# A hybrid decoder layer on one core: the second query block enters the opening, and the two parts of h become one product

## The chip, the cores and the metric

The kernel runs on one core of one Trainium2 chip. The metric is device time in microseconds (us); lower is better. Three runs of the kernel before gave 1751.47, 1755.07 and 1756.98 us, median 1755.07.

## The reference

One decoder layer for 256 tokens (two tiles of 128) of width 2048, all in float32. Cut to what matters here:

```python
mod = silu(c) @ w_ada + b_ada                       # w_ada is 2048 x 12288
sh1, sc1, g1, sh2, sc2, g2 = split(mod, 6)
h = rmsnorm(x, norm1_g) * (1 + sc1) + sh1
sq, sk, sv, cq, ckv, kr = split(h @ w_in, ...)      # 1024, 1024, 1024, 512, 256, 64 columns
sb_out  = stick_breaking_attention(sq, sk, sv)      # 8 heads of 128
q       = rmsnorm(cq) @ w_uq;  kv = rmsnorm(ckv) @ w_ukv
mla_out = mla_attention(q, kv, rope(kr))            # 8 heads
x = x + g1 * (concat(rmsnorm(sb_out), rmsnorm(mla_out)) @ w_o)
h2 = rmsnorm(x, norm2_g) * (1 + sc2) + sh2
x = x + g2 * peer_ffn(h2, ...)                      # top-16 experts of 16384 for 8 heads, gathered rows
return rmsnorm(x, final_norm_g)
```

`w_ada`, 100 MB, is read once. Its first two parts (sh1, sc1) are needed before h exists; the other four only later.

## The kernel before

Each engine runs one instruction list, written out in program order, and waits on semaphores. SP (SyncE) issues most loads, POOL (GpSimd) the late parts of `w_ada` and the expert gathers. Nothing is scheduled automatically; a few hand-written tables (`ada_after`, `ADA_IN`, `ADA_OUT`, `evicted`) say beside which weight pair some side work is done.

**The opening.** h can't be formed before sh1 and sc1 are known, and these need 33.5 MB of `w_ada`. So the kernel works in four quarters j of 512 columns. For each quarter the VectorE (DVE) adds up 16 pieces of 512 KB (`first_step`, lines 483 and 486: accumulator = piece times one value of c, plus accumulator). The TensorE (PE) then sums over partitions by products with a column of ones (`summed_columns`, line 498), DVE forms the shift and gain (`gained`), DVE and the ScalarE (ACT) apply them to four chunks of the transposed activations hT, and PE multiplies these four chunks with four chunks of `w_in` for every item of `OPENING`: the latents cq and ckv (line 876, h stationary) and the query block q0 (line 882, weights stationary). These are plain float32 products. The PSUM banks of the items stay open over the four quarters. `w_in` arrives in `opened` buffers, two sets of three, issued by SP among the pieces of `w_ada`. Between pieces 9 and 10 of the first quarter DVE also computes the angles of the rotary embedding (lines 1659 to 1677), and ACT takes their sine before it copies hT out of PSUM.

**The rest of the input projection.** The other items (q1, k0, k1, v0, v1, each 512 columns) come through two 32 KB ring slots in halves of 2 MB. Each item is worked in eight pairs of chunks (`Pair`). ACT casts a pair to a reduced float type (`make_high`, `win_high`, four buffers), DVE subtracts (`make_low`, line 452) and PE sums three products: high weights times high h, high weights times low h, low weights times high h. For q and k the weights are stationary and 256 tokens move (line 912, 24 products to a pair); for v the parts of h are stationary and 512 columns move (line 906, 12 to a pair). ACT may cast pair c only when PE has read pair c - 4. Beside these pairs DVE adds up the 16 pieces (1 MB each) of every later part of `w_ada` (`ada_sum`, line 322; three buffers, so POOL issues piece k when the sum of piece k - 3 is done). The table `ada_after` says after which pair. When 16 pieces are in, `ada_cols` on PE turns them into columns (line 333).

**Between projection and attention** PE transposes the latents, multiplies with `w_uq`, runs `ada_cols(3)`, then multiplies with `w_ukv`. DVE finishes pieces 59 to 63 before `ada_cols(3)`, and pieces 64 to 70 (up to `ADA_IN` = 71) before it may start on attention.

**Attention and output projection.** Sixteen half-head jobs run in a software pipeline; after the last one PE still sums squares for the group norm (`squares`, line 1030). The output projection is again eight pairs for each of four column blocks n (line 1069), with the same cast, subtract and multiply, and pieces 71 to 85 of `w_ada` are added on DVE, two of them before the first pair and none else in block n = 0. `rs_g` (line 1922) is the first step of the group norm on DVE; it waits for all squares.

**The retrieval** (from about 500 us on) gathers the experts' rows. The change touches nothing in it.

## Time and profile before

| | |
|---|---|
| median of 3 runs | 1755.07 us |
| the profiled execution | 1751.18 us |
| its span | 1749.4 us |
| PE busy | 1478.3 us (85%) |
| DVE busy | 1206.5 us (69%) |
| ACT busy | 542.8 us (31%) |
| POOL busy | 690.7 us (39%) |
| opening ends, projection by pairs starts | 149 us |
| projection ends | 268 us |
| first attention step of DVE | 313 us |
| output projection on PE | 363 to 462 us |

The shares are means over stages with different limits: in the opening the transfers run without a pause, in the projections PE does, and in the retrieval it is mostly the gathers. So a change in an early stage must be read from the waits of that stage. A busy PE is no PE at its peak, since its matmuls are pipelined. All times below are from the span's start.

### The profile page before, as it was taken

To read this page: it belongs to the slowest core of one execution; us is meant where nothing else is said; L and a number is where in the kernel's file an instruction comes from. 1 tells how busy PE (TensorE), PEld (TensorE's weight loads), DVE (VectorE), ACT (ScalarE), POOL (GpSimd) and SP (SyncE) were. 2 spreads that over 40 slices of the span, in tenths; PEclk is the share of its full clock that TensorE was granted. 3 is DMA by queue.
4 is the path that set the end of the run, shared out by engine and by line. 5 is a ranking of instruction groups with operands and counts; after the bars stand their busy time and mean duration, and the time that the engine had idled before them with its cause. 6 is when DMAs were issued, how large, how long until landed. Compare 5 with 4: busy or idle time off the path is not lost.

```text
span 1749.4 us, 20157 instructions
## 1 busy us (share of the span) xinstructions
PE 1478.3 (85%) x7320; PEld 980.5 (56%) x7320; DVE 1206.5 (69%) x2134; ACT 542.8 (31%) x1589; POOL 690.7 (39%) x626
## 2 busy tenths in 40 slices
PE   2979999989999998898999757656689899988874
PEld 2558987878788875666676434324333343333331
DVE  5877886879889988898454467768654555445463
ACT  3003442764311247343210146537421010101132
POOL 1000011000122354556676466555654454445461
PEclk9889999999999999999999876667789999998987
DMA  9999997849969679999999899998989999999996
GB/s 337 386 385 407 402 354 308 303 167 370 380 233 359 225 293 379 377 368 397 390 402 396 325 388 379 378 350 319 394 338 406 366 402 400 362 417 389 416 381 249
DMA packets 149806, 624.46 MB, mean 357 GB/s; under 512 B 33994, under 2 KB 38272, under 8 KB 86528
## 3 DMA queue, kind: packets, MB, share of 16 engines
q0 software_dynamic: 82976, 427.52, 62.6%
q1 hardware_dynamic: 66732, 195.67, 29.1%
q8 instruction: 58, 0.95, 0.2%
q14 instruction: 40, 0.33, 0.0%
HBM read 797.54 MB, written 2.10 MB: 457 GB/s over the span
## 4 chain that ended last, share of the span: by engine, by line
PE 31%; DMA 30%; DVE 24%; issue 6%; POOL 5%; ACT 3%; DVEq 1%; SPq 1%; POOLq 0%; ACTq 0%
DMA u_rows<-in_peer_u,expert 23%; DVE u_rows L2033 12%; PE ps L1167 6%; PE ps L1069 5%; PE ps L457 4%; PE ps L912 4%; DVE first_acc L486 3%; DMA v_rows<-in_peer_v,expert_rows 3%; POOL v_rows L801 3%; PE ps L906 2%; PE ps L1219 2%; PE ps L1134 2%; DMA ada_first<-in_w_ada 2%; PE ps L1204 2%; DMA u_rows<-in_peer_v,expert_rows 1%
## 5 line engine op out<-in xcount | busy, mean ns | idle before, releaser
L2033 DVE SCALAR_TENSOR_TENSOR u_rows<-u_rows,h 128x1024 f32<-128x1024 f32 (+1 forms) x416 | 595.3, 1469 | 377.9 <-DMA u_rows<-in_peer_u,expert 374.3
L801 POOL DMA_INDIRECT u_rows<-in_peer_u,expert x256 | 320.6, 1253 | 364.5 <-DVE u_rows L2033 289.5
L801 POOL DMA_INDIRECT v_rows<-in_peer_v,expert_rows x199 | 264.1, 1327 | 162.3 <-PE ps L1167 108.5
L1167 PE MATMUL ps<-v_rows,diag 128*32 128x512 f32 x1592 | 259.4, 693 | 65.1 <-DMA v_rows<-in_peer_v,expert_rows 35.6
L1219 PE MATMUL ps<-dense_rows,dense_weight 128*128 128x512 f32 x640 | 290.6, 612 | 14.9 <-DVE dense_sums L2112 8.2
L457 PE MATMUL ps<-h2T,dense_rows 128*128 128x256 f32 x1280 | 284.0, 383 | 4.2 <-ACT dense_weight L1565 4.1
L457 PEld LDWEIGHTS ps<-h2T,dense_rows 128*128 128x128 f32 x1280 | 243.4, 191 | 52.6 <-issue 17.9
L1219 PEld LDWEIGHTS ps<-dense_rows,dense_weight 128*128 128x128 f32 x640 | 123.1, 196 | 181.9 <-issue 174.9
L1167 PEld LDWEIGHTS ps<-v_rows,diag 128*32 128x32 f32 x1592 | 64.9, 125 | 182.5 <-issue 182.0
L308 POOL DMA_DIRECT2D ada_late<-in_w_ada x61 | 32.4, 531 | 303.7 <-DVE ada_acc L322 260.8
L1204 PE MATMUL ps<-high_hot,low_hot 128*128 128x40 f32 x512 | 82.1, 332 | 78.7 <-issue 54.0
L322 DVE SCALAR_TENSOR_TENSOR ada_acc<-ada_late,cact,ada_acc 128x2048 f32<-128x2048 f32 x57 | 133.8, 2348 | 18.8 <-DMA ada_late<-in_w_ada 17.7
L1167 PE MATMUL ps<-spare_rows,diag 128*32 128x512 f32 x296 | 135.7, 673 | 9.7 <-DMA v_rows<-in_peer_v,expert_rows 9.7
L1204 PEld LDWEIGHTS ps<-high_hot,low_hot 128*128 128x128 f32 x512 | 78.9, 244 | 95.0 <-issue 95.0
L1134 PE MATMUL ps<-h2T,ring 128*128 128x256 f32 x512 | 114.2, 383 | 0.0
L1134 PEld LDWEIGHTS ps<-h2T,ring 128*128 128x128 f32 x512 | 97.4, 192 | 13.0
L1487 ACT ACTIVATE hidden<-hidden 128x16 f32<-128x16 f32 x15 | 3.2, 215 | 314.6 <-DVE hidden L2041 311.5
L1576 ACT ACTIVATE low_hot<-iota,slot_rows 128x128 f32<-128x128 f32 x256 | 78.1, 387 | 41.1 <-PE ps L1204 40.9
L486 DVE SCALAR_TENSOR_TENSOR first_acc<-ada_first,cact,first_acc 128x1024 f32<-128x1024 f32 x60 | 77.0, 1284 | 16.1 <-DMA ada_first<-in_w_ada 10.8
L1509 ACT COPY weight_rows<-kept 32x4 f32<-32x4 f32 x240 | 47.1, 196 | 109.4 <-DVE kept L2058 106.7
L1561 ACT ACTIVATE diag<-ident,weight_rows 128x32 f32<-128x32 f32 x256 | 58.6, 308 | 40.0 <-PE ps L1167 39.4
L448 ACT CAST win_high<-ring 128x1024 fp32r<-128x1024 f32 x40 | 41.8, 1052 | 74.4 <-DMA ring<-in_w_in 32.0
(308 smaller groups left out, 1874.1 us busy)
## 6 DMA issues: line engine op xcount, KB each, us to landing
ada_late<-in_w_ada POOLq DMA_DIRECT2D x61, 1024.0 KB, 7.8
dense_rows<-in_dense_u SPq DMA_DIRECT2D x40, 1024.0 KB, 8.9
dense_rows<-in_dense_v SPq DMA_DIRECT2D x40, 1024.0 KB, 9.0
ada_first<-in_w_ada SPq DMA_DIRECT2D x64, 512.0 KB, 11.6
ring<-in_w_in SPq DMA_DIRECT2D x10, 2048.0 KB, 23.8
ring<-in_w_o SPq DMA_DIRECT2D x8, 2048.0 KB, 16.8
ring<-in_w_peer_q SPq DMA_DIRECT2D x8, 2048.0 KB, 13.8
opened<-in_w_in SPq DMA_DIRECT2D x8, 1024.0 KB, 13.0
```

The source lines that it names most:

```text
L322: nc.vector.scalar_tensor_tensor(out=a, in0=piece, scalar=cact[:, kc:kc + 1], in1=a, op0=ALU.mult, op1=ALU.add).then_inc(ada_steps, 1)
L457: ins = nc.tensor.matmul(half, lhs(k), rhs(k), start=(k == 0), stop=(k == kc - 1))
L486: nc.vector.scalar_tensor_tensor(out=a, in0=piece, scalar=cact[:, kc:kc + 1], in1=a, op0=ALU.mult, op1=ALU.add).then_inc(first_steps, 1)
L801: nc.gpsimd.indirect_dma_start(buf[:, :], None, table, bass.IndirectOffsetOnAxis(ap=places, axis=0), bounds_check=last_sparse, oob_is_err= ...
L912: ins = nc.tensor.matmul(banks[b // 2][:, T * (b % 2):T * (b % 2) + T], w.of(part, k, P * b, P), h[:, ch, :], start=first and b % 2 == 0, ...
L1069: ins = nc.tensor.matmul(banks[t], mixed[:, h, P * t:P * t + P], w.of(part, k), start=h % H == 0 and part is w.high and mixed is mix_high_ ...
L1134: ins = nc.tensor.matmul(bank[:, T * s:T * s + T], ring[item[name][0]][:, lo:lo + P], h2T[:, ch, :], start=(ch == 0 and s == 0), stop=(ch ...
L1167: ins = nc.tensor.matmul(ps[rows, k, :], diag[n % len(diag)][:, :], v_slot(n)[0][:, 512 * k:512 * k + 512], start=first, stop=last)
L1204: ins = nc.tensor.matmul(o, low_hot[i % 2][:, k, :], high_hot[i % 2][:, k, :], start=True, stop=True)
L1219: ins = nc.tensor.matmul(ps[:, 4 + t, :], weight_tile(PIECE * m + a)[:, P * t:P * t + P], rows[:, 512 * a:512 * a + 512], start=m == 0 and ...
L1576: ins = nc.scalar.activation(hot[:, k, :], iota128[:, :], ACT.Abs, scale=-1.0, bias=slot_rows[:, 1, BATCH * b + k:BATCH * b + k + 1])
L2033: ins = nc.vector.scalar_tensor_tensor(out=u_rows[b][:, lo:hi], in0=u_rows[b][:, lo:hi], scalar=1.0, in1=h2[:, q // H, lo:hi], op0=ALU.mul ...
```

## The change

What it does:

- q1 joins `OPENING`. Its products are plain float32 and are issued after those of q0 in each quarter (16 more in each). Its weights get four buffers of their own (`opened_late`, in ring slot 0), so they are loaded among the pieces of `w_ada`. Only k0, k1, v0 and v1 are left for the pairs: 32 pairs in place of 40.
- All eight PSUM banks are now taken by the opening's items, so the column sums go into 32 columns of the bank of ckv that its 320 columns leave free.
- `hT_high` and `hT_low` are two halves of one tile `h_parts`. For k0 and k1 one product with 512 moving columns (high and low h side by side) takes the place of two with 256. The two results stand in the two halves of a bank, each block of 128 output rows has its own bank, and DVE adds the halves when it evicts (`heads_out`, a reduction), where ACT copied before.
- The rotary angles move on DVE from the first quarter into the second one's pieces, and the sine on ACT after the second quarter's h.
- `ADA_IN` is 67 (was 71). Of the pieces 32 to 85, DVE does 3 before the first pair (was 2), 18 beside the pairs (was 25), 11 after the last pair (was 5), 3 before attention (was 7) and 19 in the output projection (was 15): three of the four added there stand in block n = 0, one in n = 1.
- The squares of the last two jobs are summed on PE after the first two pairs of the output projection, no longer before it.

```diff
-    OPENING = ("cq", "ckv", "q0")
+    OPENING = ("cq", "ckv", "q0", "q1")
-    ADA_IN, ADA_OUT = 71, 86
-    ada_after = {c: (37 + (c - 4) * 11 // 18, 37 + (c - 3) * 11 // 18) for c in range(4, 22)}
-    ada_after.update({c: (48 + (c - 25) * 11 // 15, 48 + (c - 24) * 11 // 15) for c in range(25, 40)})
+    ADA_IN, ADA_OUT = 67, 86
+    ada_after = {c: (35 + c * 13 // 22, 35 + (c + 1) * 13 // 22) for c in range(22)}
+    ada_after.update({c: (48 + (c - 25) * 5 // 7, 48 + (c - 24) * 5 // 7) for c in range(25, 32)})
...
     def first_bank(j):
-        return ps[:, 7 - j % 2, :]
+        return ps[:, unit["ckv_0"][0], 512 - 2 * KC:512]
...
+                            else:
+                                for b in range(4):
+                                    if part is w.high:
+                                        ins = nc.tensor.matmul(banks[b].rearrange("p (s n) -> p s n", s=2), w.of(part, k, P * b, P),
+                                                               h_parts[:, :, ch, :], start=first, stop=False, skip_group_check=True)
+                                    else:
+                                        ins = nc.tensor.matmul(banks[b][:, 0:T], w.of(part, k, P * b, P), hT_high[:, ch, :],
+                                                               start=False, stop=last, skip_group_check=True)
...
-            for k in range(JOBS + 6):
+            for k in range(JOBS + 4):
                 for stage, j in steps(k, (0, scores), (6, squares), (4, values), (2, middle)):
                     stage(j)
...
+                    if n == 0 and m < 2:
+                        squares(JOBS - 2 + m)
                     if n == 0 and m == 1:
                         gate_rows()
...
+            def heads_out(name, b):
+                dst = sbq if name[0] == "q" else sbk
+                parts = full(dve, f"{name}_{b}").rearrange("p (s n) -> p n s", s=2)
+                empty(nc.vector.tensor_reduce(dst[:, 4 * int(name[1]) + b, :], parts, AX.X, ALU.add), f"{name}_{b}")
...
+                    if n in (1, 2) and 3 <= m < 7:
+                        heads_out(IN_ITEMS[3 + n][0], m - 3)
...
-            ada_sums(59, 64)
+            ada_sums(53, 64)
...
-                    if (n, m) in ((1, 0), (1, 1), (1, 2), (1, 6), (1, 7), (2, 0), (2, 1), (2, 6), (2, 7), (3, 0), (3, 1), (3, 2), (3, 3)):
+                    if (n, m) in ((0, 3), (0, 6), (0, 7), (1, 0), (1, 1), (1, 2), (1, 3), (1, 6), (1, 7), (2, 0), (2, 1), (2, 6), (2, 7), (3, 0), (3, 1), (3, 2), (3, 3)):
                         ada_sum(next(ada))
```

Where instructions moved, first on DVE in the first quarter of the opening, before (`trig` is the rotary table, `first_acc` the accumulator; the numbers behind names count tiles):

```order
L486 SCALAR_TENSOR_TENSOR first_acc_77<-ada_first_72,cact,first_acc_77 128x1024
L1659 CAST st<-posi 128x2
L1661 TENSOR_SCALAR trig<-trig,st 128x32 x2
L1668 TENSOR_SCALAR trig<-trig 128x64
...
L1677 TENSOR_SCALAR trig<-trig 128x64
L486 SCALAR_TENSOR_TENSOR first_acc_77<-ada_first_73,cact,first_acc_77 128x1024
```

and now:

```order
L496 SCALAR_TENSOR_TENSOR first_acc_76<-ada_first_71,cact,first_acc_76 128x1024
L496 SCALAR_TENSOR_TENSOR first_acc_76<-ada_first_72,cact,first_acc_76 128x1024
...
L1711 TENSOR_TENSOR modc<-ps,vcA 128x2x4
L1715 SCALAR_TENSOR_TENSOR a1c<-modc,vcA 128x4
...
L496 SCALAR_TENSOR_TENSOR first_acc_77<-ada_first_75,cact,first_acc_77 128x1024
L1682 CAST st<-posi 128x2
L1684 TENSOR_SCALAR trig<-trig,st 128x32 x2
```

The rotary steps stood between two pieces of the first quarter and now stand behind the first shift and gain (`modc`, `a1c`), among the pieces of the second quarter.

Next on DVE where the output projection begins, before (`mix_low_part` is the low part of the attention output, `wo_high` the cast weights, `rs_g` the group norm):

```order
L452 TENSOR_TENSOR ring_low_119<-ring_49,wo_high_124 128x1024
L1922 TENSOR_SCALAR rs_g<-ps 128x4
L1874 TENSOR_TENSOR mix_low_part<-mix,mix_high_part 128x512
L452 TENSOR_TENSOR ring_low_119<-ring_49,wo_high_125 128x1024
L1874 TENSOR_TENSOR mix_low_part<-mix,mix_high_part 128x512
L452 TENSOR_TENSOR ring_low_119<-ring_49,wo_high_126 128x1024
L1874 TENSOR_TENSOR mix_low_part<-mix,mix_high_part 128x512
L452 TENSOR_TENSOR ring_low_119<-ring_49,wo_high_123 128x1024
```

and now:

```order
L460 TENSOR_TENSOR ring_low_122<-ring_49,wo_high_127 128x1024
L1948 TENSOR_SCALAR rs_g<-ps 128x4
L1900 TENSOR_TENSOR mix_low_part<-mix,mix_high_part 128x512
L460 TENSOR_TENSOR ring_low_122<-ring_49,wo_high_128 128x1024
L1900 TENSOR_TENSOR mix_low_part<-mix,mix_high_part 128x512
L460 TENSOR_TENSOR ring_low_122<-ring_49,wo_high_129 128x1024
L323 SCALAR_TENSOR_TENSOR ada_acc<-ada_late_89,cact,ada_acc 128x2048
L1900 TENSOR_TENSOR mix_low_part<-mix,mix_high_part 128x512
L460 TENSOR_TENSOR ring_low_122<-ring_49,wo_high_126 128x1024
```

`rs_g` keeps its place behind the second pair, and a piece of `w_ada` has come in behind the fourth.

Last on PE at the same place, before (`sq` holds the squares, line 1044 the rows of g1):

```order
L1030 MATMUL ps<-ones,sq 128x1 x4
L1069 MATMUL ps<-wo_high_123,mix_high_part 128x512 x2
...
L1069 MATMUL ps<-ring_low_119,mix_high_part 128x512 x4
L1069 MATMUL ps<-wo_high_124,mix_high_part 128x512 x2
...
L1069 MATMUL ps<-ring_low_119,mix_high_part 128x512 x4
L1044 MATMUL ps<-ident,modc 128x128 x16
```

and now:

```order
L1084 MATMUL ps<-wo_high_126,mix_high_part 128x512 x2
...
L1084 MATMUL ps<-ring_low_122,mix_high_part 128x512 x4
L1045 MATMUL ps<-ones,sq 128x1 x2
L1084 MATMUL ps<-wo_high_127,mix_high_part 128x512 x2
...
L1084 MATMUL ps<-ring_low_122,mix_high_part 128x512 x4
L1045 MATMUL ps<-ones,sq 128x1 x2
L1059 MATMUL ps<-ident,modc 128x128 x16
```

The last squares, for which `rs_g` waits, now come behind the products of the second pair.

## Rows read from the trace of the kernel before

**Rows 1.** Busy time by stretch: all engines, granted clock, DMA share, GB/s.
```profile
100.00:120.00 20.00, 18.62 (x63) 12.04 (x61) 16.08 (x14) 0.00 (x0) 0.00 (x0) 0.94 1.05 386
```
**Rows 2.** PE in order of time, opening: start, us, line, operation, idle before.
```profile
40.44 3.57 PE L498 MATMUL ps<-ones,first_acc 128*128 128x1 f32 x16 [5.83 <-DVE first_acc L486]
45.55 14.15 PE L876 MATMUL ps<-opened,hT 128*128 128x512 f32 x32 [1.53 <-DVE hT L1732]
...
66.94 1.95 PE L498 MATMUL ps<-ones,first_acc 128*128 128x1 f32 x16 [0.34 <-DVE first_acc L486]
70.20 13.11 PE L876 MATMUL ps<-opened,hT 128*128 128x512 f32 x32 [1.32 <-DVE hT L1732]
83.15 7.07 PE L882 MATMUL ps<-hT,opened 128*128 128x256 f32 x32
...
123.55 3.57 PE L498 MATMUL ps<-ones,first_acc 128*128 128x1 f32 x16 [4.93 <-DVE first_acc L486]
128.72 13.53 PE L876 MATMUL ps<-opened,hT 128*128 128x512 f32 x32 [1.59 <-DVE hT L1732]
```
**Rows 3.** DVE in order of time, opening.
```profile
27.81 0.16 DVE L1659 CAST st<-posi 128x2 f32<-128x2 int32 x1
...
32.15 8.23 DVE L486 SCALAR_TENSOR_TENSOR first_acc<-ada_first,cact,first_acc 128x1024 f32<-128x1024 f32 x6
...
109.71 13.78 DVE L486 SCALAR_TENSOR_TENSOR first_acc<-ada_first,cact,first_acc 128x1024 f32<-128x1024 f32 x10 [2.60 <-DMA ada_first<-in_w_ada]
```
**Rows 4.** The chain that ended last, in order of time: start, us, what.
```profile
149.15 66.23 PE ps L912 x552
215.38 3.84 PE ps L333 x32
219.22 5.33 PE ps L912 x24
224.55 43.65 PE ps L906 x191
...
291.95 3.48 PE ps L333 x32
...
371.48 3.57 PE ps L1044 x32
375.05 46.31 PE ps L1069 x204
```
**Rows 5.** A reduction of 512 PSUM columns on DVE, in order of time.
```profile
534.22 0.69 DVE L1999 TENSOR_REDUCE halves<-ps 128x32 f32<-128x512 f32 x1
```
**Rows 6.** DVE in order of time, end of the projection.
```profile
252.09 2.35 DVE L452 TENSOR_TENSOR ring_low<-ring,win_high 128x1024 fp32r<-128x1024 f32 x2
...
259.29 2.35 DVE L322 SCALAR_TENSOR_TENSOR ada_acc<-ada_late,cact,ada_acc 128x2048 f32<-128x2048 f32 x1 [1.45 <-DMA ada_late<-in_w_ada]
...
282.78 2.35 DVE L322 SCALAR_TENSOR_TENSOR ada_acc<-ada_late,cact,ada_acc 128x2048 f32<-128x2048 f32 x1 [0.21 <-DMA ada_late<-in_w_ada]
```
**Rows 7.** PE in order of time, first scores of attention.
```profile
310.00 0.60 PE L988 MATMUL ps<-sbq,sbk 128*128 128x256 f32 x2
```
**Rows 8.** DVE in order of time, before attention.
```profile
310.66 2.35 DVE L322 SCALAR_TENSOR_TENSOR ada_acc<-ada_late,cact,ada_acc 128x2048 f32<-128x2048 f32 x1 [0.43 <-DMA ada_late<-in_w_ada]
312.93 0.55 DVE L1810 SCALAR_TENSOR_TENSOR za<-za 128x384 f32<-128x384 f32 x1
```
**Rows 9.** DVE in order of time, output projection.
```profile
364.86 0.15 DVE L1922 TENSOR_SCALAR rs_g<-ps 128x4 f32<-128x4 f32 x1
...
376.29 0.69 DVE L1874 TENSOR_TENSOR mix_low_part<-mix,mix_high_part 128x512 fp32r<-128x512 f32 x1 [6.07 <-ACT mix_high_part L1434]
...
383.51 1.23 DVE L452 TENSOR_TENSOR ring_low<-ring,wo_high 128x1024 fp32r<-128x1024 f32 x1 [1.37 <-ACT wo_high L448]
...
414.69 2.35 DVE L322 SCALAR_TENSOR_TENSOR ada_acc<-ada_late,cact,ada_acc 128x2048 f32<-128x2048 f32 x1 [1.93 <-DMA ada_late<-in_w_ada]
416.96 3.49 DVE L452 TENSOR_TENSOR ring_low<-ring,wo_high 128x1024 fp32r<-128x1024 f32 x3
```

More of the change, by code:

```diff
@@ L327, in ada_sums, with ada_bank @@
             ada_sum(k)
+    def ada_bank(part):
+        return ps[:, 3 if part == 2 else 7, :]
     def ada_cols(part):
@@ L701, in _ @@
                 if j < 3:
-                    for i in range(9, KC):
+                    for i in range(12, KC):
                         first_load(sp, KC * (j + 1) + i)
-            for name, col, width in IN_ITEMS[3:]:
-                if name == IN_ITEMS[4][0]:
+            for name, col, width in IN_ITEMS[4:]:
+                if name == "k0":
                     sp.wait_ge(first_steps, 4 * KC)
@@ L859, in _ @@
                 fill(ins, f"xT{u}")
+            banks = {name: [take(pe, f"{name}_{i}") for i in range(2)] for name in OPENING}
             summed_columns(0)
-            banks = {name: [take(pe, f"{name}_{i}") for i in range(2)] for name in OPENING}
             for j in range(4):
@@ L876, in _ @@
                                 ins = nc.tensor.matmul(banks[name][t][:, 0:width], hT[:, ch, P * t:P * t + P], w[:, ch % 4, 0:width],
-                                                       start=(ch == 0), stop=last)
+                                                       start=(ch == 0 and (name, t) != ("ckv", 0)), stop=last, skip_group_check=True)
                                 if last:
@@ L890, in _ @@
                     summed_columns(j + 1)
-            for n, (name, _, width) in enumerate(IN_ITEMS[3:]):
-                banks = [take(pe, f"{name}_{i}") for i in range(2)]
+            for n, (name, _, width) in enumerate(IN_ITEMS[4:]):
+                banks = [take(pe, f"{name}_{i}") for i in range(2 if name[0] == "v" else 4)]
                 for m in range(PAIRS):
@@ L1746, in _ @@
                 if j:
[L1747 removed]
+                    opened_read_through(dve, j - 1, 3)
                     h_parted(j - 1)
@@ L1751, in _ @@
                         first_step(j + 1, kc)
+                        if j == 0 and kc == 11:
+                            trig_args()
                 else:
                     opened_read_through(dve, 3, 0)
-                    ada_sums(32, 34)
-            for n, (name, _, width) in enumerate(IN_ITEMS[3:]):
+                    ada_sums(32, 35)
+            for n, (name, _, width) in enumerate(IN_ITEMS[4:]):
                 for m in range(PAIRS):
```

149 lines of the change are left out of this document (76 added, 73 removed).

## The prediction

> **What bounds the kernel now.** I read the stretches first, then the chain of waits, then each engine in order of time where the change touches it. Three stages matter.
>
> The opening, 7 to 149 us, runs at the pace of its transfers: the DMA share is 1.05 at 386 GB/s [rows 1]. PE is idle before every quarter's column sums, 4.93 us before the last ones, and always until DVE has added its last piece [rows 2]; DVE in turn waited 2.60 us for a piece, then added ten in a row [rows 3]. So a load that is put in front of a piece delays the end of the stage, while more products on PE cost nothing as long as they fit into the gap.
>
> The projection, 149 to 268 us, belongs to PE: on the chain stand 576 products of 256 columns, 16 ones-products and 192 products of 512 columns without a wait [rows 4]. DVE keeps up with it, and also loses time to late pieces there [rows 6].
>
> From 268 to 462 us PE and DVE take turns. Attention begins when DVE is through its pieces of `w_ada` [rows 8], and the output projection is PE's again, with DVE close behind it [rows 4, 9]. The retrieval after that is untouched and follows the shift of its start, so I cost it at nothing.
>
> The sum is made against the profiled execution: span 1749.4 us, time 1751.18, so 1.8 us lie around the span. The median of the runs shown is 3.9 us above it. I add the change to the median.
>
> **The opening, with the rotary steps moved: ends 14.0 us later.** First the start. The six last pieces of the first quarter start at 32.15 where the rotary steps began at 27.81 [rows 3]. These steps leave, and so does ACT's wait for them before it copies hT. The column sums can start 4.3 us earlier than at 40.44, the first products at 41.2 in place of 45.55 [rows 2]. The pieces must have landed for that, which I take since six were then added without a wait. The moved steps fall beside PE's first quarter, where DVE has room.
>
> Now PE's pace. A quarter took 12.95 us for the latents (70.20 to 83.15) and 7.07 us for a query block; between the end of the products and the next quarter lie 3.6 us (0.3 to the column sums, then 66.94 to 70.20) [rows 2]. With two query blocks a quarter costs 12.95 + 14.14 + 3.6 = 30.7 us, the first one 31.9 (its latents took 14.15 us). From 41.2 the quarters start at 73.1, 103.8 and 134.5.
>
> And the transfers' pace. Three chunks of q1 (1.05 MB each) come ahead of the last piece: 3.15 MB at 386 GB/s are 8.2 us. The last column sums go from 123.55 to 131.7 at the earliest, the last quarter from 128.72 to 136.9, or 135.3 if PE is not slowed by its gap. Both paces come out within 2 us of each other; I take the slower one, 136, and 27.1 us of products: the opening ends at 163.1, before it ended at 149.15. Ends: 161.6 (PE alone) and 166 (both add up in part). h_parts for the last quarter and the casts of k0 run beside the next pairs, four of which are ready ahead; its weights wait, as before, for the last piece, and have 30 us to land.
>
> **The projection: 24.6 us shorter on PE.** q1 leaves it. 552 products of 256 columns took 66.23 us, 0.120 us each [rows 4]; q1 has 192: 23.0 us. In k0 and k1, 128 products of 512 columns replace 256 of 256. The v products took 43.65 us for 192, 0.227 us each, so the doubled width costs 0.107 us more and each product has 0.013 us that doesn't depend on width: 128 times 0.013 is 1.6 us saved. No row shows a moving operand in two pieces. If it streams like one, the gain is 1.6; if at half rate, 128 times 0.227 = 29 us are lost. Every operand here is read at the column rate, so I take 1.6 and keep the 29 for a rival. The Trainium skill (TensorE: Matmul & The Clock Gate, Back-to-back issue gap) puts the width-free part of a product at about 2.5 ns; by that figure the merge would save 0.3 us (an estimate from that page) and the forecast would be 1.3 us higher. The row's 13 ns disagrees with it here.
>
> Together: 14.0 - 23.0 - 1.6 = **-10.6 us** when the v products end, at 257.6.
>
> **DVE beside it: 0.** A pair costs DVE 1.16 us, a piece 2.27 (414.69 to 416.96) [rows 9]. With 13 pieces to 22 pairs that is 2.50 us to a pair. The reductions that replace ACT's copies are 8; the nearest row is a reduction of 512 PSUM columns in 0.69 us [rows 5], between 0.6 and, if the stride of 256 halved its rate, 1.4. Four to eight pairs make 0.35, in all 2.85 us against PE's 64 x (0.227 + 0.120) / 8 = 2.78. DVE falls back 0.1 us a pair over 16 pairs, and the cast buffers give it a lead of four pairs less some 3 us. Hidden; 0 to +4 if it isn't.
>
> **`ada_cols(3)`: +1.5.** PE reached it at 291.95, 23.7 us after the v products [rows 4]; the last piece was done at 285.13 [rows 6], 6.8 us in hand. Now PE arrives at 281.3. DVE leaves the pairs near 251 (the four pairs it is ahead by, less the cast), with 11 pieces to add, not 5: at 2.35 us each done at 277, at the pace of the last eight before (259.29 to 285.13, 3.23 us each, limited by landing) at 286.5. So 0 to +5.2. Loads are no more in total, hence a value near the lower end.
>
> **The start of attention: -1.5.** PE had the first scores at 310.6 [rows 7]; with one scaling on ACT between, for which I put 0.8 us, DVE could begin at 311.4. It began at 312.93, straight after a piece [rows 8]. Three pieces stand there now, all loaded during the wait for `ada_cols(3)`; what is late next is the scores. Running sum -10.6.
>
> **The output projection: +6.0, given back.** DVE did `rs_g` at 364.86 [rows 9]. Its wait is new in kind: the last squares stand behind PE's second pair, which ended at 371.48 [rows 4]. `rs_g` is held for 6.9 us, and behind it on DVE stand the low parts of all further pairs. PE itself isn't stopped, since the 3.57 us of g1 rows cover the third pair. Then come four pieces, 9.1 us, before pair 18. Of these 16.0 us, DVE's idle stretches take up 6.07, 1.37 and 1.93 [rows 9], and the margin of pair 18 takes 0.5 (low part ready near 418.1; PE's 17 pairs from 375.05 take 46.31 us, 2.72 each, so it started it at 418.6). Left are 16.0 - 9.4 - 0.5 = 6.1, less a little where g1's rows shift too: 6.0. The column sums behind pair 18 give DVE room again, but it then ran as tightly as before, so nothing of it comes back. Bounds: 0, if DVE's lead is larger than I read it, to +8, if the wait for the transfer isn't absorbed. The squares leaving the end of attention give nothing: DVE's two pieces set that start.
>
> **Sum.** -10.6 + 1.5 - 1.5 + 6.0 = **-4.6 us**: 1746.6 on the profiled execution, **1750.5 us** on the median.
>
> **Rivals.**
> - *Nothing is given back.* The output projection stays PE's, as 9.4 us of idle DVE would suggest at first sight; against it speaks the margin of 0.5 us at pair 18. -4.6 - 6.0 = -10.6: 1744.5 us.
> - *Small waits eat the rest.* Pieces land every 3.23 us as they did at the end of the projection: +3.7 at `ada_cols(3)`, and 2 us in the pairs and the opening. +1.1: 1756.2 us. For it: DVE waited for pieces in all three stages [rows 3, 6, 9]. Against: the bytes are the same.
> - *DVE becomes the bound of the projection, and the kernel slower.* Place: the 17 pieces between the pairs from the end of the opening on. If each waits 1.45 us, as the one at 259.29 did [rows 6], that is 24.6 us; the lead of the cast buffers takes 8.5: +16.1, in sum +11.5: 1766.6 us. It decides from (9.9 + 8.5) / 17 = 1.1 us a piece. Against it: before, most pieces there came without a wait, though the queues were as full.
> - *The two-piece operand streams at half rate:* -4.6 + 29 + 1.6 = +26: 1781 us. It is slower from 0.08 us a product.
>
> **Numbers.** 0.3% is 5.3 us, about what a measurement of this kernel tells from no change. My own forecast 0.49, with its own range 1746 to 1754; it straddles the bound, so 0.26 of it is faster and 0.23 within. No giveback 0.18 (faster), small waits 0.20 (within), DVE bound 0.10 and half rate 0.03 (slower). Faster 0.44, same 0.43, slower 0.13. The range reaches past both near rivals, and part of the way to the third: 1741 to 1761.
>
> **What would show it.** Opening: first latents at 41, quarters near 73, 104 and 136, products of q1 ending near 163; a last quarter after 140 breaks that step. Projection: 128 products of 512 columns at 0.227 us for k0 and k1, no idle PE up to 258; idle PE until `ring_low` means DVE is the bound. `ada_cols(3)` at 281 to 287, first DVE step of attention near 302. Output projection: `rs_g` waiting near 7 us for the squares, and PE idle for 0.5 to 0.8 us before pairs 11 to 18, 6 us in all. If those idles are absent, the gain is the full one.

## The result, and the profile after

The changed kernel takes 1769.52 us (median of 4 runs, 1766.57 to 1776.05), the kernel before 1753.69 us (4 runs): ratio 1.0094, 95% interval [1.0066, 1.0121]. It is slower by 0.9%, where 1750.5 us and a range up to 1761 had been forecast. The profiled execution (span 1774.3 us) is the slowest of the four, 6.5 us above their median. Its span is 24.9 us longer than that of the trace before; 17.4 of these have arisen when the retrieval begins and 7.5 lie in the retrieval, which the change doesn't touch. So stages are compared only up to its start.

The opening, PE in order of time, against [rows 2] (start, us, line, operation, idle before):

```profile
41.19 13.76 PE L885 MATMUL ps<-opened,hT 128*128 128x512 f32 x32 [1.52 <-DVE hT L1753]
...
72.72 3.15 PE L508 MATMUL ps<-ones,first_acc 128*128 128x1 f32 x16 [3.96 <-DVE first_acc L496]
77.19 12.83 PE L885 MATMUL ps<-opened,hT 128*128 128x512 f32 x32 [1.32 <-DVE hT L1753]
...
137.02 13.11 PE L885 MATMUL ps<-opened,hT 128*128 128x512 f32 x32 [1.59 <-DVE hT L1753]
149.96 7.07 PE L891 MATMUL ps<-hT,opened 128*128 128x256 f32 x32
156.87 7.07 PE L891 MATMUL ps<-hT,opened_late 128*128 128x256 f32 x32
```

It starts at 41.19 and ends at 163.6, as forecast (41.2 and 163.1). In between, the second quarter is late, 77.2 for 73.1, since PE waited 3.96 us for its last piece; the other two start at 106.8 and 137.0 for 103.8 and 136. The transfers are as full as in [rows 1]:

```profile
100.00:120.00 20.00, 18.68 (x68) 11.96 (x67) 13.33 (x16) 2.12 (x4) 0.00 (x0) 0.91 1.05 385
```

From the end of the pairs to attention, PE, against [rows 4, 7]:

```profile
258.86 1.03 PE L941 MATMUL ps<-ident,lat 128*128 128x128 f32 x8
...
293.83 6.96 PE L337 MATMUL ps<-ones,ada_acc 128*128 128x1 f32 x32 [11.29 <-DVE ada_acc L323]
300.65 9.46 PE L465 MATMUL ps<-ckvT,ring 128*128 128x256 f32 x32
309.95 7.03 PE L465 MATMUL ps<-ring,ckvT 128*128 128x512 f32 x16
316.81 1.04 PE L994 MATMUL ps<-ident,qpe 128*128 128x128 f32 x8
317.69 0.60 PE L1003 MATMUL ps<-sbq,sbk 128*128 128x256 f32 x2
```

The pairs end at 258.9 (before 268.3): 9.4 us gained. Then PE waits 11.3 us for the last piece that part 3 of `w_ada` needs. After the wait even its own work is slower. In the kernel before, the same column sums took 3.63 us and the first `w_ukv` products 7.15, here 6.96 and 9.46; before:

```profile
291.78 3.63 PE L333 MATMUL ps<-ones,ada_acc 128*128 128x1 f32 x32
295.27 7.15 PE L457 MATMUL ps<-ckvT,ring 128*128 128x256 f32 x32
```
 The granted clock of the changed kernel shows why (columns as in [rows 1]; of the last three the first is the clock, as a share of full speed):

```profile
280.00:285.00 5.00, 2.54 (x6) 0.76 (x4) 4.18 (x2) 0.00 (x0) 0.53 (x1) 0.98 0.92 331
285.00:290.00 5.00, 0.00 (x0) 0.00 (x0) 2.87 (x2) 0.00 (x0) 1.06 (x2) 0.50 0.91 339
290.00:295.00 5.00, 1.17 (x6) 1.20 (x6) 3.60 (x5) 0.00 (x0) 0.53 (x1) 0.50 0.77 275
295.00:300.00 5.00, 5.00 (x25) 5.00 (x25) 3.39 (x9) 0.00 (x0) 0.00 (x0) 0.50 0.65 213
```

0.50 is the lower of the two levels, 1.2 GHz. The clock fell to it while PE was idle and rose again only after 305 us.

DVE beside it, against [rows 6, 8]: the pieces come at the pace of their landing, eleven of them take 39.9 us from 253.76 on, 3.63 us each, and attention waits for the scores:

```profile
271.32 2.35 DVE L323 SCALAR_TENSOR_TENSOR ada_acc<-ada_late,cact,ada_acc 128x2048 f32<-128x2048 f32 x1 [5.15 <-DMA ada_late<-in_w_ada]
...
291.33 2.35 DVE L323 SCALAR_TENSOR_TENSOR ada_acc<-ada_late,cact,ada_acc 128x2048 f32<-128x2048 f32 x1 [2.21 <-DMA ada_late<-in_w_ada]
...
319.07 0.56 DVE L1836 SCALAR_TENSOR_TENSOR za<-za 128x384 f32<-128x384 f32 x1 [11.86 <-ACT za L1385]
```

A good half of the wait has its cause further back, as e5 shows. Between 228 and 236 us the transfers almost stop:

```profile
220.00:228.00 8.00, 8.00 (x40) 6.68 (x39) 6.45 (x6) 5.08 (x7) 0.53 (x1) 1.00 1.03 406
228.00:236.00 8.00, 8.00 (x39) 7.13 (x39) 2.50 (x3) 0.43 (x1) 0.53 (x1) 0.64 0.13 42
```
```profile
231.94 0.17 DVE L347 TENSOR_TENSOR modc<-ps,vcA 128x16 f32<-128x16 f32 x1 [5.20 <-PE ps L337]
```

DVE has added piece 47, casts up to pair 25 and then waits 5.2 us for `ada_cols(2)`, before which it may not begin the next part. All three piece buffers are full, and both ring slots wait for PE. In the kernel before DVE waited 2.57 us for the same sums, but the transfers went on at 383 GB/s from 212 to 228 us.

The output projection, against [rows 9] (waits: engine, what, releaser, us in all, times, longest), and PE's longest wait behind the first pair (the 4.5 us stand before that pair):

```profile
PE ps L1084 <- DVE ring_low L460: 9.4, 10, 4.5
...
DVE rs_g L1948 <- PE ps L1045: 6.9, 1, 6.9
```
```profile
412.00 0.70 PE L1084 MATMUL ps<-wo_high,mix_high_part 128*128 128x512 f32 x2 [1.94 <-DVE ring_low L460]
...
435.39 4.03 PE L337 MATMUL ps<-ones,ada_acc 128*128 128x1 f32 x32
```

From its first product to the end of the last key rows it takes 110.0 us (369.5 to 479.5), before 98.8 (363.35 to 462.1).

The balance up to the retrieval, after minus before: end of the pairs -9.4; wait for the piece +11.3; column sums and first `w_ukv` products at the lower clock +3.3 and +2.3; start of attention behind the scores -1.5; output projection +11.2. These terms make +17.2. The transposes behind it begin at 483.7 against 466.3: **+17.4 us**. The medians differ by 15.8.

### The profile page after: what moved, and what is told of

Read it like the earlier page. It is cut to its first block, busy times and chain, and to the rows that moved or that the text cites. A ratio compares the mean times of both kernels' runs of the same rounds, so it can differ in the third digit from the quotient of the medians.

```text
span 1774.3 us, 19763 instructions
## 1 busy us (share of the span) xinstructions
PE 1488.6 (84%) x7128; PEld 978.6 (55%) x7128; DVE 1202.5 (68%) x2134; ACT 534.1 (30%) x1577; POOL 692.5 (39%) x626
## 4 chain that ended last, share of the span: by engine, by line
PE 26%; DMA 24%; DVE 14%; issue 6%; POOL 6%; ACT 1%; DVEq 1%; POOLq 0%; ACTq 0%
DMA u_rows<-in_peer_u,expert 16%; DVE u_rows L2059 8%; PE ps L1184 8%; PE ps L1236 7%; DMA v_rows<-in_peer_v,expert_rows 5%; POOL v_rows L811 4%; PE ps L465 3%; PE ps L1084 2%; PE ps L1151 2%; PE ps L1221 2%; POOL u_rows L811 1%; DMA ada_late<-in_w_ada 1%; DMA u_rows<-in_peer_v,expert_rows 1%; DVEq L1979 1%; DVE tk_i L1987 1%
## 5 line engine op out<-in xcount | busy, mean ns | idle before, releaser
L811 POOL DMA_INDIRECT u_rows<-in_peer_u,expert x256 | 324.3, 1267 | 366.6 <-DVE u_rows L2059 291.4
L1236 PE MATMUL ps<-dense_rows,dense_weight 128*128 128x512 f32 x640 | 288.8, 609 | 15.8 <-DVE dense_sums L2138 9.2
L1184 PE MATMUL ps<-spare_rows,diag 128*32 128x512 f32 x296 | 139.7, 694 | 9.5 <-DMA v_rows<-in_peer_v,expert_rows 9.5
L1184 PEld LDWEIGHTS ps<-spare_rows,diag 128*32 128x32 f32 x296 | 29.7, 125 | 53.1 <-issue 52.9
```

What stands on the lines that cost most here:

```text
L811: nc.gpsimd.indirect_dma_start(buf[:, :], None, table, bass.IndirectOffsetOnAxis(ap=places, axis=0), bounds_check=last_sparse, oob_is_err= ...
L1184: ins = nc.tensor.matmul(ps[rows, k, :], diag[n % len(diag)][:, :], v_slot(n)[0][:, 512 * k:512 * k + 512], start=first, stop=last)
L1236: ins = nc.tensor.matmul(ps[:, 4 + t, :], weight_tile(PIECE * m + a)[:, P * t:P * t + P], rows[:, 512 * a:512 * a + 512], start=m == 0 and ...
```

## Experiments

The marks of the kernels that were run more than once, from their traces (us). "Stage" is from the end of the pairs to DVE's first attention step; "w_o" from the output projection's first product to the last key rows; "retrieval" is when the transposes ahead of it begin. The marks show more than the medians can, since the retrieval's own length varied by over 10 us between traces (1277.8 us in e5, 1290.6 in the changed kernel). But each kernel has one trace, and the end of the pairs alone differs by up to 5 us between kernels that are alike up to there, so a difference of a few us between two rows is not shown to come from the edit. The ratio is to the kernel before on the same chip, whose medians were 1752.27 (e1 to e4), 1748.40 (e5 to e8), 1754.15 (e9 to e12) and 1753.57 us (e13, b1).

| kernel | pairs end | PE waits | column sums, next products | first step | stage | w_o | retrieval | ratio, 95% |
|---|---|---|---|---|---|---|---|---|
| before | 268.3 | 0 | 3.63, 7.15 | 312.9 | 44.7 | 98.8 | 466.3 | 1 |
| after | 258.9 | 11.3 | 6.96, 9.46 | 319.1 | 60.2 | 110.0 | 483.7 | 1.0094 |
| e1 sums last | 255.6 | 5.4 | 3.63 | 310.2 | 54.6 | 108.4 | 474.6 | 1.0067 [1.0041, 1.0094] |
| e2 squares back | 254.9 | 11.3 | 6.96, 8.94 | 314.6 | 59.7 | 106.5 | 475.6 | 1.0096 [1.0065, 1.0128] |
| e3 pieces back | 259.8 | 12.0 | 6.96, 8.89 | 320.2 | 60.4 | 100.4 | 475.2 | 1.0036 [1.0011, 1.0062] |
| e4 small fill | 256.5 | 0.7 | 5.17, 9.03 | 313.7 | 57.2 | 107.5 | 475.9 | 1.0094 [1.0064, 1.0124] |
| e5 first sums early | 257.2 | 4.9 | 6.96, 9.61 | 311.2 | 54.0 | 108.3 | 474.1 | 1.0101 [1.0061, 1.0141] |
| e6 sums between | 258.1 | 3.8 | 6.96, 9.67 (wide) | 311.0 | 52.9 | 108.5 | 474.1 | 1.0050 [1.0029, 1.0070] |
| e9 joined, two back | 263.9 | 0 | 3.63, 8.81 (wide) | 309.6 | 45.7 | 102.3 | 466.4 | 0.9989 [0.9966, 1.0012] |
| e12 joined, four back | 257.5 | 0 | 4.69, 9.48 (wide) | 312.7 | 55.2 | 98.5 | 467.2 | 1.0025 [0.9999, 1.0050] |
| e13 e9, sums spread | 260.7 | 1.7 | spread | 318.7 | 58.0 | 103.9 | 478.1 | 1.0067 [1.0043, 1.0091] |
| b1 before, sums spread | 268.8 | 0 | spread | 322.9 | 54.1 | 98.5 | 477.4 | 1.0072 [1.0047, 1.0097] |

"Wide" are the 16 products of 512 columns, 7.03 us at full clock.

**The wait ahead of `ada_cols(3)`: e1, e6.** PE waits there for DVE's last piece, and everything behind it waits too.

```diff
 # e1: behind both halves of the w_ukv products; e6: between them
-            ada_cols(3)
             w = group(pe, "w_ukv", 2 * n_in, KVR // P)
             ...
+            ada_cols(3)
```


> The changed kernel, with `ada_cols(3)` moved on PE behind the `w_ukv` products. Theory (the column sums wait for late pieces, and everything behind them with them): PE goes from `w_uq` to `w_ukv` without a wait at about 282.5 and is through near 296, the column sums wait little, the first scores come near 302 and DVE's first attention step, after its last three pieces, near 307.5 instead of 319.1. The kernel gains 11 to 12 us on the changed kernel: about 1758 us. Rival 1 (DVE's own pieces and rotary work set the start of attention anyway): the start moves by 5 us or less, 1764 to 1768. Rival 2 (the loss at this place is given back later): the start moves by 11 us and the time by less than 5.

The stage got 5.6 us shorter, not 11, near rival 1 in size; 1763.86 us. The mechanism is another one than rival 1 had. PE found a new wait, for banks that DVE's rotary work held, and DVE then waited 9.5 us for the sums:

```profile
291.59 8.82 PE L465 MATMUL ps<-ring,ckvT 128*128 128x512 f32 x16 [5.41 <-DVE rt L1815]
300.25 3.63 PE L337 MATMUL ps<-ones,ada_acc 128*128 128x1 f32 x32
303.74 1.07 PE L994 MATMUL ps<-ident,qpe 128*128 128x128 f32 x8
```


> The changed kernel, with `ada_cols(3)` between the two halves of the `w_ukv` products (behind the 32 of 256 columns, ahead of the 16 of 512). Where the sums stood behind both halves, the second half waited 5.4 us for banks that DVE's rotary work held, and DVE then waited 9.5 us for the sums. Theory (both waits come from that order alone): PE waits about 4 to 5 us for the sums, the second half runs beside the rotary work, the first attention step comes 46 to 48 us after the end of the projection's pairs, where the changed kernel has 60.2, the order with the sums last 54.6 and the kernel before 44.7: about 1757 us. Rival (what is missing is the pieces' landing): 54 us again, 1764.

52.9 us, 7.3 less than after and 5 to 7 more than expected. Both waits went as foreseen (PE 3.8 us, DVE 2.3), but the clock fell behind the 3.8 us just as behind 11.3: 6.96 us for the sums, 9.67 for the wide products. The lower clock costs 6.0 us here, about the size of the miss. Median 1758.98 us (about 1757 expected).

**The pause of the transfers: e5.**

```diff
-                    if w.c == 22:
+                    if w.c == 20:
                         copied(pe, "k0_3")
                         ada_cols(2)
 # DVE: ada_finish(2) at pair 23, pieces 48 to 54 beside pairs 24 to 31, ada_sums(55, 64) behind
```


> The changed kernel, with `ada_cols(2)` on PE two pairs earlier (after pair 20, when its last piece has been added), and the first pieces of the next part from pair 24 on, 7 of them beside the pairs in place of 5. Theory (the transfers stood still from 228 to 236 us because all three buffers of `w_ada` were full and DVE waited for these column sums; that pause, and not DVE's work, is why piece 63 comes 8 us later than in the kernel before): the pause goes or shrinks to 3 us, the last piece ahead of `ada_cols(3)` is done 5 to 6 us earlier, PE's wait there shrinks from 11.3 us to 5 or 6, attention starts as much earlier: 1762 to 1764 us. Rival (the pieces come at the pace of the queue and the pause is made up behind it): the last piece moves by 2 us or less and the time stays within 2 us of 1769.5.

The theory on the pause holds in the trace. The same stretch moved 189 GB/s in place of 42, and PE's wait shrank by 6.4 us, from 11.29 to 4.89. What is left of it has the pieces' pace: the last eleven took 38.3 us here too, 3.48 us each, from 247.3 on.

```profile
228.00:236.00 8.00, 8.00 (x34) 6.54 (x33) 6.09 (x5) 3.16 (x3) 1.06 (x2) 0.92 0.60 189
```
```profile
285.76 6.96 PE L337 MATMUL ps<-ones,ada_acc 128*128 128x1 f32 x32 [4.89 <-DVE ada_acc L323]
```

The stage is 6.2 us shorter and the retrieval begins 9.6 us earlier (1.7 of it from pairs that ended earlier). The time doesn't show it: the median is 1767.35 us (1762 to 1764 expected) and the ratio, 1.0101, no better than the changed kernel's 1.0094. The five runs reach from 1753.62 to 1771.39 us, and the profiled one is the fastest.

**The output projection: e2, e3.**

```diff
 # e2
-            for k in range(JOBS + 4):
+            for k in range(JOBS + 6):
 ...
-                    if n == 0 and m < 2:
-                        squares(JOBS - 2 + m)
```


> The changed kernel, with the last two `squares` back at the end of attention, so that `rs_g` doesn't wait. Theory (the 6.9 us in which `rs_g` holds DVE are paid by PE later in the output projection, because DVE's slack is used up by the four more pieces): the output projection gets 5 to 7 us shorter up to pair 18, less 0.5 at its start: about 1764 us. Rival (the wait is absorbed by DVE's idle time, the loss comes from the four pieces alone): 0 to -2, 1768 to 1770.

w_o 106.5: 3.5 us shorter, between the theory (5 to 7) and the rival (0 to 2). `rs_g` doesn't wait, but PE still idles before seven pairs. Median 1768.65 us, which is the rival's number (1768 to 1770) and not the theory's 1764.

```diff
 # e3
-    ADA_IN, ADA_OUT = 67, 86
+    ADA_IN, ADA_OUT = 71, 86
-                    if (n, m) in ((0, 3), (0, 6), (0, 7), (1, 0), (1, 1), (1, 2), (1, 3), (1, 6), ...
+                    if (n, m) in ((1, 0), (1, 1), (1, 2), (1, 6), ...
```


> The changed kernel, with the four pieces of `w_ada` that it added to the output projection's block 0 and 1 back ahead of attention (`ADA_IN` 71). Theory: ahead of attention they fit into the time in which DVE waits for the first scores (it was idle from 307 to 317.7, four pieces cost 9.1 us), so attention starts at most 1 us later; in the output projection DVE gets 9.1 us of slack and PE's idle before pairs 11 to 18 disappears: -8 to -9 us, about 1761 us. Rival 1 (`rs_g`'s wait alone makes the idle): -2 or less, 1767 to 1770. Rival 2 (the pieces land too late ahead of attention, at 3.6 us each): attention starts 4 to 5 us later, in sum -4.

The theory came true. Attention starts 0.2 us later relative to the pairs (its four pieces were added while DVE waited for the scores), w_o is 9.6 us shorter, and PE waits before no pair but the first:

```profile
317.13 2.35 DVE L323 SCALAR_TENSOR_TENSOR ada_acc<-ada_late,cact,ada_acc 128x2048 f32<-128x2048 f32 x1 [0.46 <-DMA ada_late<-in_w_ada]
320.18 0.56 DVE L1836 SCALAR_TENSOR_TENSOR za<-za 128x384 f32<-128x384 f32 x1 [0.70 <-ACT za L1385]
```

Median 1760.88 us (about 1761 expected). With both edits (e12) w_o is 98.5 us, the 98.8 of before: the four pieces and the squares are the whole loss there, the pieces the larger part.

**The clock behind the wait: e4, e7, e11.** In all three PE does work in the wait whose result nobody reads.

```diff
 # e4: 44 products of 128 x 128; e7: 12 of 128 x 512 with cqT; e11: 14 of these
             copied(pe, "v1_1")
+            for _ in range(44):
+                nc.tensor.matmul(ps[:, 7, 128:256], ident[:, :], ident[:, :], start=True, stop=True)
             ada_cols(3)
 # e11 also: no row of sums, but two of them behind each group of four first w_ukv products
```


> The changed kernel, with 44 idle products (128 x 128, on a bank that nobody reads) on PE in the 11.3 us in which it waits for the pieces ahead of `ada_cols(3)`. The output is the same. Theory (the idle stretch lowers the granted clock, and the column sums and the `w_ukv` products behind it run slowly for that alone): the column sums take 3.6 to 4.4 us instead of 6.96, the products of `w_ukv` 7.2 to 7.5 instead of 9.46, the first scores come 4 to 5.5 us earlier: about 1764.5 us. Rival (they are slow for another reason, such as loads that collide with them): the durations stay and the time stays within 1 us of 1769.5.

> The changed kernel, with 12 idle products of 128 x 512 (the shape of the `w_uq` products before them) in PE's wait ahead of `ada_cols(3)`. With 88 small ones there the clock stayed at 1.00 in the gap and still fell to 0.55 to 0.77 behind it. Theory (the small products don't keep the clock up, the wide ones do): column sums 3.6 us, `w_ukv` products 7.15 and 7.03, the stage from the pairs' end to the first attention step 54 to 55 us in place of 60.2. Rival (the clock falls behind the gap whatever fills it, with the column sums themselves): 57 us, as with the small ones.

Neither theory. In e4 the clock stayed up in the gap and fell behind it, the stage was 3.0 us shorter, the median 1767.74 us and the ratio that of the changed kernel, 1.0094. In e7 12 wide products left 1.84 us of wait, and the sums took 6.56 us, the next products 9.28; its stage was 60.5 us, time 1769.33 (one run). Both in stretches of 5 us, first e4, then e7:

```profile
285.00:290.00 5.00, 5.00 (x46) 4.84 (x44) 4.66 (x3) 0.00 (x0) 1.05 (x2) 1.00 0.74 256
290.00:295.00 5.00, 4.34 (x30) 4.31 (x29) 4.79 (x12) 0.00 (x0) 0.53 (x1) 0.77 1.01 415
295.00:300.00 5.00, 5.00 (x16) 4.23 (x16) 4.29 (x6) 0.48 (x1) 0.53 (x1) 0.55 0.31 85
```
```profile
290.00:295.00 5.00, 3.16 (x12) 1.46 (x10) 3.07 (x4) 0.00 (x0) 0.46 (x1) 0.98 0.73 290
295.00:300.00 5.00, 5.00 (x25) 5.00 (x25) 3.92 (x10) 0.00 (x0) 0.07 (x1) 0.50 0.63 213
```


> The changed kernel, with 14 wide idle products in PE's wait (12 left a gap of 1.8 us) and the column sums of `ada_cols(3)` spread between the first `w_ukv` products, two behind each group of four, in place of sixteen in a row. Theory (with the gap filled, the column sums themselves, one column each, make the clock fall): from the first of them to the last `w_ukv` product PE takes 18 us, at a clock of 1.00, where the changed kernel takes 23.1 (6.96 + 9.46 + 7.03 less the overlaps) and the kernel before 17.5; first attention step 55 us behind the end of the pairs. Rival (what remains of the gap is enough for the clock to fall): 22 to 23 us again.

Here nothing of the wait was left and the clock stayed at 1.00; from the first `w_ukv` product to the transposes 17.35 us (expected 18), stage 55.1, time 1761.52 (one run):

```profile
290.00:295.00 5.00, 5.00 (x29) 4.36 (x28) 4.27 (x11) 0.58 (x1) 0.45 (x1) 1.00 0.65 216
295.00:300.00 5.00, 5.00 (x32) 4.61 (x32) 0.00 (x0) 1.17 (x2) 0.00 (x0) 1.00 0.02 8
```

So about 5.1 us of the 15.5 that the stage grew by come from the lower clock. e11 changed two things, though: it left no gap, and it had no row of sums. Which of them kept the clock up is taken up again with e13.

**The merged product and the rotary steps: e8, e10** (one run each).

```diff
 # e8
-   ins = nc.tensor.matmul(banks[b].rearrange("p (s n) -> p s n", s=2), w.of(part, k, P * b, P), h_parts[:, :, ch, :], ...)
+   for s in range(2):
+       ins = nc.tensor.matmul(banks[b][:, T * s:T * s + T], w.of(part, k, P * b, P), h_parts[:, s, ch, :], start=first and s == 0, ...)
```


> The changed kernel, with the merged product of k0 and k1 taken apart again: two products of 256 columns in place of one of 512, in the same banks and with the same reductions. Theory (a product has 0.013 us that don't depend on its width): a pair of k0 or k1 costs 2.89 us in place of 2.79, the pairs end 1.6 us later. Rival by the width-free part of 2.5 ns: 0.3 us later. Rival by half rate: the pairs end 27 us earlier, which the 1.85 us for eight merged products already speak against.

From the first pair to `ada_cols(2)`, 23 pairs, it took 66.35 us less 0.9 of idle; e11 and e2, with one product, took 63.95 and 63.95 without idle: 1.5 us, as the row of before had said. Time 1763.62.

```diff
 # e10: DVE
-            for kc in range(7, KC):
+            for kc in range(7, 10):
                 first_step(0, kc)
+            trig_args()
+            for kc in range(10, KC):
+                first_step(0, kc)
 # ACT's sine again ahead of the copies of hT
```


> The changed kernel, with the rotary steps back in the middle of the first quarter's pieces, and ACT's sine ahead of its copies. The opening otherwise as changed. Theory (the opening ends at the pace of its transfers, so the rotary steps' place only moves the idle time): the first products start 3 to 4.5 us later, near 45, the second quarter near 77 as now, the opening ends within 1 us of 163.6. Rival (PE's pace sets the end): it ends 3 to 4 us later, near 167.

First products at 45.74, second quarter 75.66, end of the opening 162.7 (after: 163.6). The steps' place is worth nothing: what the changed kernel gains at the start it loses in the 3.96 us for which its second quarter waits. With the later start PE waited for the pieces only 0.42 us, at the last quarter's sums: in this order PE's own pace (29.9 us a quarter) and that of the transfers end the opening together. Time 1775.70.

**Joined: e9, e12.** The edits of e5, e6 and e2, and `ADA_IN` 69 or 71.

> Four edits on the changed kernel together: `ada_cols(2)` two pairs earlier, `ada_cols(3)` between the halves of the `w_ukv` products, the last squares back at the end of attention, and two of the four pieces moved back ahead of attention (`ADA_IN` 69). Theory (the changed kernel lost in the two places where PE and DVE meet, and what its opening and projection gained is kept once these are mended): the pieces are done when PE needs the sums, so PE doesn't wait there and the clock stays up; the first attention step comes 44 to 46 us after the end of the pairs (60.2 in the changed kernel), the output projection from its first product to the last key rows takes about 100 us (110.0; before 98.8): the retrieval begins near 459 where it begins at 483.7 in the changed kernel and at 466.3 before. About 1746 us, 0.3 to 0.5% faster than the kernel before. Rival (the transfers bound the stage up to attention, so that it can't start earlier than before): 1752, no difference.

Stage 45.7 and no wait of PE, as the theory said. The clock didn't stay up, though: behind the sums, which nothing had delayed, the wide products took 8.81 us for 7.03. w_o 102.3, 2.3 longer than it said. The retrieval begins at 466.4 and not near 459, because this kernel's pairs ended at 263.9 (which also gave the pieces time to land, so the short stage is in part owed to it): DVE was late at two pairs (1.93 and 1.47 us), and `ada_cols(2)`, now close behind piece 47, waited and ran slowly:

```profile
225.43 5.94 PE L337 MATMUL ps<-ones,ada_acc 128*128 128x1 f32 x32 [1.63 <-DVE ada_acc L323]
```

1751.22 us (12 runs) and a ratio of 0.9989 [0.9966, 1.0012]: 1% faster than the changed kernel, but no different from the kernel before, which is the rival's outcome (1752).

> The same four edits, but with all four pieces ahead of attention (`ADA_IN` 71). Theory: attention starts 4.6 us later than with two of them (2.3 us a piece, DVE has no idle time there any more), the output projection gains 1 us or less: 3.5 to 4.5 us more than with two. Rival (DVE is still the later one in the output projection, with 0.5 us before several pairs): equal.

1758.57 us. The stage grew by 9.5 us (4.6 expected): its pairs ended 6.4 us earlier than those of e9, but the pieces land no faster (one waited 2.89 us), so attention started 3.1 us later. w_o shrank by 3.7. The retrieval starts within 0.8 us of that of e9; no trace shows why the medians are 7.4 us apart.

**The row of column sums: e13, b1.** e13 is e9 with both rows of sums spread; b1 is the kernel before with them spread.

```diff
 # e13: beside the products of pair 21; b1: of pair 23, one at a time
-                        ada_cols(2)
+                                        for o in (next(cols, None), next(cols, None)):
+                                            if o is not None:
+                                                col = ada_col(2, o)
```


> The four edits of the joined kernel with two pieces back, and the column sums of both parts spread between wide products: those of `ada_cols(2)` two behind each of the first eight products of pair 21, those of `ada_cols(3)` four behind each group of the second half of `w_ukv`. Theory (sixteen column sums in a row let the granted clock fall behind them, which costs 0 to 5 us at the first place, differently from run to run, and 2 us or more at the second): the clock stays at 1.00 from 163 to 310 us, the pairs end at 255 to 256, the first scores come 42 us behind that, attention starts at 300 to 302 and the retrieval begins 6 to 8 us earlier than at 466.4: 1744 to 1746 us, faster than both. Rival (DVE's pieces bound the start of attention, 45.7 us behind the pairs' end whatever PE's clock): 1748 to 1750 us.

> The kernel before, with the column sums of both parts spread likewise: those of `ada_cols(2)` between the products of pair 23, those of `ada_cols(3)` between the first `w_ukv` products. Theory: the projection ends up to 3 us earlier where the clock fell behind `ada_cols(2)` (0.92 in its trace), but attention's start is set by DVE's pieces, which come at the pace of landing: 0 to -3 us, so that what the joined kernel gains by it isn't to be had here alone. Rival (the clock's fall costs nothing that isn't hidden): 0.

Both theories fell. Expected were 1744 to 1746 us for e13 and a gain of 0 to 3 us for b1. e13: 1764.80 us, ratio 1.0067 [1.0043, 1.0091]. The clock was 0.66 from 223 to 238 us with spread sums too, behind a wait of 1.66 us at 222.2; the pairs ended at 260.7. b1: 1766.36 us, 1.0072 [1.0047, 1.0097], and the clock behind the first sums the same as before (0.91 for 0.93 from 223 to 238 us). So at the first sums the clock falls without the row too. At the second ones the question stays open: with spread sums the clock stayed at 1.00 in e11, in b1 and in e13, there even behind a wait of 1.70 us, while with the row it fell in e7 behind 1.84 us and in e9 and e12 behind no wait at all, but not in the kernel before or in e1. What both lost shows how much hangs on the sums: until they are complete DVE may not begin the next part, the buffers stay full and the transfers stand (b1 moved 69 GB/s from 290 to 300 us and 144 from 300 to 310, the kernel before 44 and 392). DVE waited 7.80 us for the second sums in e13 and 7.85 in b1, where it had them at 302.9 in place of 295.5:

```profile
302.92 0.17 DVE L347 TENSOR_TENSOR modc<-ps,vcA 128x16 f32<-128x16 f32 x1 [7.85 <-PE ps L338]
303.03 1.28 DVE L319 TENSOR_SCALAR ada_acc<-ada_late,cact 128x2048 f32<-128x2048 f32 x1
...
320.61 2.35 DVE L322 SCALAR_TENSOR_TENSOR ada_acc<-ada_late,cact,ada_acc 128x2048 f32<-128x2048 f32 x1 [2.37 <-DMA ada_late<-in_w_ada]
322.87 0.55 DVE L1824 SCALAR_TENSOR_TENSOR za<-za 128x384 f32<-128x384 f32 x1
```

Attention started at 322.9, 9.9 us later, although PE had the scores at 310.5. It is a pause of the same kind as the one that e5 shortened.

## Why the prediction was wrong

- *Opening, +14.0:* right in size, 163.6 for 163.1, with some luck in the path. The wait for the transfers was expected before the last quarter and came before the second, which was 4 us late; the later quarters then took 29.6 and 30.2 us where 30.7 had been put, so that the last one started only 1.0 us late. PE waited for no piece ahead of it.
- *Projection, -24.6:* right. The pairs ended at 258.9 for 257.6, and at 254.9 to 259.8 in the other kernels with this order. The merged product brought 1.5 us for 1.6, 12 ns a product over 128 products (e8), and two pieces of a moving operand stream like one (eight such products took 2.00 us, eight with one piece 1.98). The Trainium skill (TensorE: Matmul & The Clock Gate, Back-to-back issue gap) gives about 2.5 ns a product, which would make 0.3 us, an estimate from that page. It gives the figure for an isolated product, though, and says that it under-counts at small widths where each product has its own weight load. In this kernel each has one (39 loads to 40 products from 220 to 228 us), which the prediction left out when it compared the two. DVE beside the pairs: at most small waits (none here, up to 3.4 us in sum in e9).
- *`ada_cols(3)`, +1.5 with bounds 0 to +5.2:* the step that failed. It measured +11.3 us of wait and, as a term that the prediction didn't have, +5.6 us of lower clock behind it. The pace was taken as 2.35 to 3.23 us a piece, near the lower end on the ground that the loads are no more in total, and the upper value is misread: from 259.29 to 285.13 the kernel before added seven pieces, not eight. These stand between the two lines of [rows 6]:

```profile
263.89 2.35 DVE L322 SCALAR_TENSOR_TENSOR ada_acc<-ada_late,cact,ada_acc 128x2048 f32<-128x2048 f32 x1 [1.12 <-DMA ada_late<-in_w_ada]
267.09 4.82 DVE L322 SCALAR_TENSOR_TENSOR ada_acc<-ada_late,cact,ada_acc 128x2048 f32<-128x2048 f32 x2 [0.85 <-DMA ada_late<-in_w_ada]
272.87 2.35 DVE L322 SCALAR_TENSOR_TENSOR ada_acc<-ada_late,cact,ada_acc 128x2048 f32<-128x2048 f32 x1 [0.96 <-DMA ada_late<-in_w_ada]
280.21 2.35 DVE L322 SCALAR_TENSOR_TENSOR ada_acc<-ada_late,cact,ada_acc 128x2048 f32<-128x2048 f32 x1 [5.00 <-DMA ada_late<-in_w_ada]
```

25.84 us for seven are 3.69 each, and with that the forecast's own way would have given 251 + 11 x 3.69 = 291.6 and a bound of +10.3. Measured were 3.63 each from 253.8 on, ready at 293.7, with PE there at 282.5. The loads before attention were as slow before; with six pieces fewer behind the pairs that was hidden. The start of this run of pieces is what the pause sets: loads can't run on when nobody empties a buffer. DVE's wait for `ada_cols(2)` stood ahead of 15 pairs before and of 7 now. e5, by moving that one point, had DVE at the pace of landing 6.4 us earlier and took 6.4 us of PE's wait away; the pace, 3.48 us there, is the rest.

- *Start of attention, -1.5:* right, to 0.1 us (first step 1.4 us behind the scores).
- *Output projection, +6.0 with bounds 0 to +8:* mechanism right, size wrong: +11.2 in all, 8.0 of it by the end of pair 18. `rs_g` waited 6.9 us as said, and PE waited ahead of the pairs 10 to 18, 4.9 us in all. Two things were missing. DVE's landing waits (1.38 us before a piece at 408.4) weren't absorbed. And the room behind pair 18, which was to bring nothing, brought a loss: `ada_cols(4)` took 4.03 us for 3.63 and the pairs 19 to 30 behind it 2.8 us more than before, with a granted clock of 0.50 from 440 to 445 us. e2, e3 and e12 confirm where it is from.
- *The rivals.* Small waits was the nearest in kind, with 5.2 us (1.5 + 3.7) for this place where 16.9 came. DVE as the bound and half rate didn't happen.

In sum: 15.4 us missed at `ada_cols(3)`, 5.2 in the output projection, 1.2 at the end of the pairs, 21.8 together. -4.6 + 21.8 = +17.2 us at the start of the retrieval, where the traces differ by 17.4; the medians, 15.8 apart, by a little less.

What stays open: the granted clock fell behind the sums of `ada_cols(2)` also where PE hadn't waited, in the kernel before (0.50 from 220 to 224 us), the changed one, e1, e3 to e7 and e10, and it stayed at 1.00 in e2, e8 and e11, though e2 and e11 run the program of the changed kernel up to there. The end of the pairs differs by up to 5 us, in part by that (254.9 in e2 and e11, 258.9 in the changed kernel), and no run says what decides it. Nor was the pause tested from its other side, with a fourth piece buffer.

## What to carry to other kernels

Where the same bytes have to arrive by a point that moves closer, follow the transfers and not the engine: look for the stretch in which buffers are full and their reader waits for a third engine, since a pause that cost nothing with slack behind it becomes the wait. A wait put on a busy engine must be priced with what runs right behind it, here half as much again as the wait itself. A pace read from a trace should be counted piece by piece, since one piece too many in eight hid 5 us of what this wait could be. And work that is taken out of one stage's idle time has to be set against the next stage's slack piece by piece: four pieces cost 9.6 us where they went and 0.2 us where they had been, as long as DVE waited there anyway (e3).

## What was not expected of the hardware

The cost of the fallen clock didn't depend on the length of the wait: 1.84, 3.76, 4.89 and 11.29 us all gave column sums of 6.6 to 7.0 us for 3.63, and 1.7 to 2.6 us on the products behind. A remainder of 0.66 us gave 5.17. Even with no wait the clock could fall behind the sums: in e9 the sums took 3.63 us and the wide products behind them 8.81 for 7.03, in e12 4.69 and 9.48. A wait filled with small products kept the clock at 1.00 in the gap, and it still fell after it.
